# Who requests the pages of the compressed cache: three engines by twelve, eight and twelve, or two by sixteen

## The reference, as far as it matters

```python
cmp_past = cache_cmp_kv[li, page_table].reshape(B, past_len, 2, G, D)
ckv = jnp.concatenate([compress_blocks(cmp_past, pe, w1, w2),
                       compress_blocks(cmp_kv, pe, w1, w2)], axis=1)
```

## Time and profile before

| | |
|---|---|
| median of three executions | 1725.9 us |
| the profiled execution | 1729.2 us |
| its span, first to last instruction | 1727.5 us |
| mean granted TensorE clock | 0.96 |
| busy in the span: PE, DVE, ACT, POOL | 1588.4, 774.2, 610.7, 754.1 us |
| moved by DMA | 213.39 MB, mean 124 GB/s |
| requests of `rows`: SyncE, GpSimd, ScalarE | 116, 84, 56, of 128 KB each |

### The profile page before, as it was taken

One profiled execution on the slowest core, in us unless ns is written; L12 is line 12 of the kernel. 1 busy time (PEld: TensorE's weight loads), 2 busy tenths in 40 slices (PEclk: granted clock), 3 DMA queues, 4 the chain that ended last, 5 costly groups with the idle time before them and its releaser, 6 DMA issues. The chain is left out here.

```text
span 1727.5 us, 35385 instructions
## 1 busy us (share of the span) xinstructions
PE 1588.4 (92%) x13664; PEld 1399.9 (81%) x13664; DVE 774.2 (45%) x1448; ACT 610.7 (35%) x1159; POOL 754.1 (44%) x523
## 2 busy tenths in 40 slices
PE   6999567898889899999999999998998999999997
PEld 6999465566656688999999988986667999999997
DVE  2210556555556587232233276146659522223235
ACT  3221333355544436322222224136434532222322
POOL 6641663433346456544344336312136644434430
PEclk9998888799999999999999999998999999999999
DMA  8435895455375352533333222224223333233211
GB/s 242 115 84 134 270 293 173 121 182 157 119 203 168 135 182 64 183 116 115 110 123 94 78 74 69 82 91 153 85 64 112 106 99 98 82 90 104 85 33 50
DMA packets 295104, 213.39 MB, mean 124 GB/s; under 512 B 33892, under 2 KB 287384, under 8 KB 294296
## 3 DMA queue, kind: packets, MB, share of 16 engines
q1 hardware_dynamic: 277448, 178.86, 34.5%
q0 software_dynamic: 8496, 22.68, 4.1%
q10 hardware_dynamic: 8992, 9.57, 2.0%
HBM read 198.85 MB, written 20.55 MB: 127 GB/s over the span
## 5 line engine op out<-in xcount | busy, mean ns | idle before, releaser
L1801 POOL TENSOR_TENSOR w_own_t<-w_raw,w_own_t 128x1024 fp32r<-128x1024 f32 (+1 forms) x82 | 194.0, 2371 | 186.5 <-ACT w_own_t L1929 186.5
L1623 PE MATMUL ps<-x_parts,w_own_t 128*128 128x512 f32 x464 | 165.0, 396 | 3.2 <-POOL w_own_t L1801 3.2
L1801 POOL TENSOR_TENSOR w_low_ahead<-w_raw,w_high_ahead 128x1024 fp32r<-128x1024 f32 (+1 forms) x40 | 94.8, 2373 | 129.6 <-ACT w_high_ahead L1929 129.5
L1910 PE MATMUL ps<-x_parts,w_own_t 128*128 128x264 f32 x464 | 132.2, 285 | 0.0
L1912 PE MATMUL ps<-x_parts,w_own_t 128*128 128x264 f32 x464 | 131.8, 284 | 0.0
L1911 PE MATMUL ps<-x_parts,w_own_t 128*128 128x264 f32 x464 | 131.8, 284 | 0.0
L1625 PE MATMUL ps<-x_parts,w_own_t 128*128 128x256 f32 x464 | 130.1, 280 | 0.0
L1929 ACT CAST w_own_t<-w_raw 128x1024 fp32r<-128x1024 f32 (+1 forms) x82 | 83.4, 1024 | 96.4 <-PE ps L1912 80.5
L2086 DVE TENSOR_REDUCE whole_t<-ps 128x256 f32<-128x512 f32 x44 | 30.4, 690 | 181.2 <-PE ps L1625 181.2
L1163 POOL TENSOR_TENSOR e<-e,rg 128x1024 f32<-128x1024 f32 (+3 forms) x48 | 66.9, 1394 | 97.3 <-DVE rg L1433 96.7
L770 PE MATMUL ps<-flat,w 64*64 64x128 f32 (+1 forms) x2048 | 73.3, 302 | 39.2 <-DVE flat L549 20.5
(11 more groups left out here) (452 smaller groups left out, 4865.3 us busy)
## 6 DMA issues: line engine op xcount, KB each, us to landing
w_raw<-in_ffn_w_gu SPq DMA_DIRECT2D x88, 512.0 KB, 3.7
pages<-in_cache_slc SPq DMA_DIRECT2D x192, 128.0 KB
rows<-in_cache_cmp SPq DMA_DIRECT2D x116, 128.0 KB, 4.5
w_raw<-in_ffn_w_down SPq DMA_DIRECT2D x32, 448.0 KB, 3.6
w_raw<-in_gla_w_in SPq DMA_DIRECT2D x24, 512.0 KB, 3.6
rows<-in_cache_cmp POOLq DMA_DIRECT2D x84, 128.0 KB, 6.2
pages<-in_cache_slc POOLq DMA_DIRECT2D x64, 128.0 KB, 2.9
w_raw<-in_ffn_w_down SPq DMA_DIRECT2D x16, 512.0 KB, 4.0
```

Of the source, the lines that this page charges most:

```text
L1623: nc.tensor.matmul(bank[:, 0:2 * FOLD].rearrange("p (a n) -> p a n", a=2), high, parts[2][:, :, at, 0:FOLD], start=(k == 0), stop=False)
L1801: nc.gpsimd.tensor_tensor(low(u)[:, 0:k], raw[:, u % RAW, 0:k], high(u)[:, 0:k].bitcast(F32), ALU.subtract).then_inc(low_done, 1)
L1910: nc.tensor.matmul(psum(i), high(u)[:, k, :], a[0][:, at, c], start=(k == 0), stop=False)
```

## The change

SyncE requests pages 0 to 15 of a unit and GpSimd pages 16 to 31; ScalarE requests none. ScalarE's `row_pages` and `load_part` calls and its semaphores are gone, and GpSimd's share has number 1 in place of 2. The number of bytes is the same, and so is the compute; ScalarE still makes chunks 2 and 6 of each unit's eight.

```diff
-ROW_SHARE = (0, 12, 20, ROW_UNIT)
+ROW_SHARE = (0, 16, ROW_UNIT)
...
             pool.wait_ge(pt_in, 16)
-            S["next_pages"][2] = row_pages(pool, S, 0, 2)
+            S["next_pages"][1] = row_pages(pool, S, 0, 1)
...
             act.wait_ge(pt_in, 16)
-            S["next_pages"][1] = row_pages(act, S, 0, 1)
             act.wait_ge(gate_pre, 2)
...
-        first_rows, other_rows = ([[sem("%s_rows_%s%d" % (some, n, s)) for s in range(2)] for n in ("sp", "act", "sw")]
+        first_rows, other_rows = ([[sem("%s_rows_%s%d" % (some, n, s)) for s in range(2)] for n in ("sp", "sw")]
...
-            for by in range(3):
+            for by in range(2):
                 for part in (first_rows, other_rows):
...
             for n in range(1, len(UN)):
-                load_part(pool, n, 2)
+                load_part(pool, n, 1)
...
                 if n == 0:
-                    load_part(act, 1, 1)
                     act.wait_ge(cst["w1_in"][1], 16)
...
-                if n + 2 < len(UN):
-                    load_part(act, n + 2, 1)
                 if n == 4:
```

## The result

The changed kernel takes 1740.5 us (median of 5 runs, 1735.6 to 1741.6) beside 1725.9 us (5 runs, 1719.4 to 1727.4) of the kernel before. The ratio is 1.0073, with a 95% interval from 1.0049 to 1.0098: slower, by 0.0073 x 1725.9 = 12.6 us. The forecast was 1728 with a range of 1717 to 1737. It missed, and so did the range.

The account below looks back on a forecast made before the run. In the compression it took SyncE's serial requests and loads as the limit once ScalarE is free: 0 (ScalarE's gain, covered) + 2.5 us (SyncE up to unit 6) took 1725.9 to 1728, range 1717 to 1737.

Parts of the forecast that it names:

- SyncE's row: Compression: SyncE's serial requests (sixteen take 9.7 us) and loads (sixteen take 9.0), said to set when units can be requested.
- S2: Earliest start of SyncE's requests for unit 2 in the compression: forecast 196.2 us, 192.0 before.
- S3: Earliest start of SyncE's requests for unit 3 in the compression: forecast 205.9 us, 208.2 before.
- S4: Earliest start of SyncE's requests for unit 4 in the compression: forecast 224.9 us, 223.9 before.
- S6: Earliest start of SyncE's requests for unit 6 in the compression: forecast 253.6 us, 251.1 before.
- The time of a unit from SyncE's request: Compression: a unit requested into empty queues is there 16.4 us later, with 2.3 to first landing and 12.6 of transfer.
- ScalarE's relief: Rival, chance 0.15: the compression shortens by TensorE's whole 11.6 us wait for ScalarE's copies, to 1714, given as 1715.
- SyncE's slack: Compression: units before the last pair were said to have slack from SyncE, so slow GpSimd requests delay only the last pair.
- The forecast's +2.5: Compression: unit 6's later request start on SyncE shifts everything behind by +2.5 us; main forecast, chance 0.50.
- GpSimd's requests: Rival, chance 0.18: GpSimd's slow requests delay unit 7 in the compression once each costs over 0.85 us; 1733 to 1735.
- r: GpSimd's time for each page request in the compression: 0.76 us mean over the stage before, deciding at 0.85.
- the forecast's own term: The +2.5 us from unit 6's later start on SyncE, bounded at +7 with dearest rows and -5 with cheapest.

Follow-up runs that it names:

- e7: The changed kernel without GpSimd's loads of page numbers inside the stage, SyncE's kept (output not the reference's): 1727.7 us, ratio 1.0003 to the kernel before.
- e2: The changed kernel without either engine's loads of page numbers inside the stage (first quarter's numbers throughout, output not the reference's): 1724.6 us, ratio 0.9993.
- e10: The kernel before without ScalarE's loads of page numbers inside the stage, its requests and copies kept (output not the reference's): 1719.2 us, ratio 0.9948.
- e15: The kernel before, shares 12, 8 and 12, with all 32 of ScalarE's page numbers loaded in the projection, computation complete: 1720.7 us, ratio 0.9963.
- e1: The changed kernel without the wait on the landed first half of an engine's own pages of the unit before: 1730.5 us, ratio 1.0022.
- e8: The changed kernel with ScalarE making three of a unit's eight copies in place of two: 1736.0 us, ratio 1.0048.
- e12: The changed kernel as in e11, with ScalarE also making three of a unit's eight copies: 1734.0 us, ratio 1.0036.
- e11: The changed kernel without the landed-half wait, three quarters' page numbers loaded ahead (SyncE's behind its stores), the last quarter's after unit 2's requests: 1729.1 us, ratio 1.0008.

## Why the prediction was wrong

**SyncE's row** was right in its prices. S2, S3, S4 and S6 came within 1.0 us, with the luck told above (a start 2.6 us early, a row 3.6 us longer); e7, where GpSimd isn't late, has them all to 0.6 us. The prediction named as a sign of being wrong that SyncE pauses over 2 us ahead of unit 4 or 6. It paused 2.1 us ahead of unit 6, behind the flattening of a unit whose rows GpSimd had brought late. The time of a unit from SyncE's request, put at 16.4 us, was 17.7 us for unit 2 (213.4 - 195.7), 22.5 for unit 4 and 24.0 for unit 6: the forecast counted from SyncE's request, as if GpSimd's half were asked for as soon. That two queues fill the DMA engines was right (349 GB/s). That the third one is worth nothing holds against the time of the kernel before (e2), but not against what three can do (e10 is 7.8 us faster than e2). One comparison there was off: it set sixteen requests and sixteen loads, 18.7 us, against the transfer of one unit, 12.6, but the loads serve two units. For a pair it is 28.7 against 25.2 us; the order stays, the margin is small.

**ScalarE's relief** was right for this change: its wait fell from 11.6 us to nothing, and nothing of it reached the end. But e10 and e15 show that relief from the loads alone is real where the rest of the change isn't made: 9.0 us and 6.4 us. In the changed kernel the later rows cover it.

**The step that failed** is the change-over from SyncE to both engines: four requests and four loads more "on SyncE and on GpSimd both" were priced, and only SyncE's row was followed. For GpSimd the prediction said "The place is the last pair of units, nowhere else, since the earlier ones have SyncE's slack." That slack isn't there. The wait of line 515 sits at each odd unit, and what it delays is handed on through the loads to the next even unit. In us behind the forecast, at the rows of each unit as VectorE got them: unit 2 0.8, unit 4 5.1, unit 6 8.6, unit 7's first copy 8.8, last product 9.8 (305.4 against 293.1 + 2.5 = 295.6). The forecast's +2.5 and the measured 12.6 us differ by 10.1; e1 takes away 8.8 us with the one line, and e7, without GpSimd's loads, 12.1 of the 12.6. In the sum GpSimd's row stood at nothing; it is worth some 10 us, by loads that make it late and a wait that then holds it.

**The rival that came nearest**, GpSimd's requests, was right in its engine and wrong in place and in its deciding number. It was to decide at 0.85 us for each request. The groups of instructions in the stage after (busy time in us, mean in ns, idle ahead), as the earlier trace rows:

```profile
L519 POOL DMA_DIRECT2D rows<-in_cache_cmp x111 | 83.9, 763 | 25.9 <-DVE flat L548 7.0 <-issue 6.7 <-ACT flat L548 6.2
```

The mean is 763 ns, the same as before to the digit. By my own test GpSimd would have been acquitted. A mean says nothing on which request is slow: a request that overlaps one of VectorE's row copies takes 1.23 us (37 of 112), one that doesn't 0.54 (75). The three over 3 us are among the first six requests of units 2, 4 and 6 (3.08, 4.64 and 3.28 us), and a wait on the first half hangs on just these. The rival also let GpSimd begin unit 6 at 254.0, with SyncE, where it began at 260.7; it priced only when the last page lands, 1733 to 1735, and left out everything that GpSimd itself waits for.

**The chances.** The mechanism that decided stood in none of the cases, and the chance of 0.17 for slower was tied to r over 1.05, which never came. The range ended at 1737, called GpSimd's price, which the rival itself puts at 1733 to 1735; the bounds of the forecast's own term, 1721 to 1734, were taken from SyncE's rows alone.

**What stays open.** How much of GpSimd's lateness is due to VectorE's copies was not isolated: e8 moved the whole by 4.3 us, not clear of noise and along with other things. The wait could only be tried by taking it out or by changing its count. What four loads more on each engine cost by themselves was not measured, nor why three requesters without ScalarE's loads (e10) are faster than two with none (e2). Why e12 is slower than e11 is argued from two traces.

## What to carry to other kernels

Where an edit puts the same work on two engines, work out the row of each, with its own waits; the one whose price is known may be the one that doesn't matter. A wait that costs nothing in the kernel before is not free in the kernel after: write down for each wait in the changed loop how much margin it has (here none was left, it held GpSimd up by 1.6 us), and follow a delay round the loop, since a queue with no slack hands it to every later turn. Before moving requests from an engine, look whether its loads of registers can move alone: here that was worth 6.4 us, and the move of the requests cost 12.6.

## What the runs showed of the hardware

- A page number loaded into a register costs 0.54 to 0.58 us of an engine's queue, on SyncE, ScalarE and GpSimd alike, nearly as much as the request that uses it (0.61). With two queues a pair of units, 8.4 MB, takes each queue 32 requests and 16 loads, 28.7 us by the forecast's prices (29.1 and 28.3 on GpSimd in e1); the DMA engines move it in 25.2 at 330 to 338 GB/s.
- GpSimd's sequencer passes requests on at 0.59 us each, while the requests proper take 0.54 us where no row copy of VectorE's overlaps, and 1.23 in the mean, up to 4.64, where one does. So the end of its row in the queue doesn't tell when the pages were asked for: in unit 4 of the changed kernel 236.0 against 240.3.
- Two queues reach the rate of three (349 GB/s from 209 to 222 after, against 338 from 191 to 206 before): the third issuer brought no bandwidth in these stretches. Over the stage it is still worth having (e10 against e2).
